# Inputs laid out by partition on the host, and the first modulation in four blocks of four, in a two-layer decoder step on one core

## The reference

```python
mod = jax.nn.silu(c) @ w_ada + b_ada
shift, scale, gate = jnp.split(mod, 3, axis=-1)
h = _rmsnorm(x, g_norm) * (1.0 + scale[:, None, :]) + shift[:, None, :]
cols = jnp.split(h @ w_in, np.cumsum(COL_SIZES)[:-1].tolist(), axis=-1)
...
y = x + gate[:, None, :] * (o @ w_out)
```

## Time and profile before

| | us |
|---|---|
| median of 3 runs | 2353.13 (2352.44 to 2353.47) |
| the profiled execution, first to last instruction (its span) | 2351.4 |
| its own time beside the span | not recorded apart from the three runs; the median lies 1.7 above the span |
| TensorE busy in the whole span | 2296.5 |
| TensorE busy in the first 126 us | 88.8 |
| start of the first pair block | 73.2 |
| end of the three first tiles (start of the next tile) | 131.8 |

### The profile page before, as it was taken

One profiled execution on the slowest core, in us unless ns is written; L12 is line 12 of the kernel. 1 busy time (PEld: TensorE's weight loads), 2 busy tenths in 40 slices (PEclk: granted clock), 3 DMA queues, 4 the chain that ended last, 5 costly groups with the idle time before them and its releaser, 6 DMA issues.

```text
span 2351.4 us, 50350 instructions
## 1 busy us (share of the span) xinstructions
PE 2296.5 (98%) x21251; PEld 2174.7 (92%) x21251; DVE 1283.2 (55%) x2499; ACT 753.7 (32%) x1219; POOL 938.6 (40%) x668
## 2 busy tenths in 40 slices
PE   5899999999999999999999999999999999999998
PEld 3799999999999999998888999999999999999998
DVE  5465666677776333442127566567767744345444
ACT  2243332333333333421114333233333333334111
POOL 2143343444333444453333333343333344346552
PEclk8999999999999999999999999999999999999999
DMA  9972333555554434368887233355554434433443
GB/s 365 352 230 76 92 92 109 156 155 155 155 155 123 114 102 110 101 194 257 247 283 215 74 92 92 92 155 155 156 158 106 125 98 109 116 95 109 109 120 107
DMA packets 473482, 347.22 MB, mean 148 GB/s; under 512 B 18701, under 2 KB 417513, under 8 KB 471937
## 3 DMA queue, kind: packets, MB, share of 16 engines
q1 hardware_dynamic: 473258, 344.02, 49.9%
HBM read 312.07 MB, written 32.09 MB: 146 GB/s over the span
## 4 chain that ended last, share of the span: by engine, by line
PE 90%; DVE 4%; DMA 3%; DVEq 1%; issue 1%; ACT 1%; POOL 1%; SPq 0%; ACTq 0%; POOLq 0%
PE pj L722 72%; PE mx L728 3%; DMA rows<-in_w_ada 2%; PE mx L1087 2%; PE mx L1113 2%; PE mx L843 1%; PE mx L1101 1%; PE mx L809 1%; PE pj L1220 1%; PE mx L1065 1%; PE mx L1115 1%; PE mx L1105 1%; DVE t L1598 1%; PE mx L990 1%; DMA rows<-in_x_prompt 1%
## 5 line engine op out<-in xcount | busy, mean ns | idle before, releaser
L722 PE MATMUL pj<-hh,whi 128*128 128x260 f32 x4928 | 1419.9, 288 | 7.9 <-DVE hl L1598 7.6
L690 POOL TENSOR_TENSOR wlo<-raw,whi 128x512 fp32r<-128x512 f32 x632 | 893.0, 1444 | 1311.7 <-ACT whi L1302 1311.7
L722 PE MATMUL pj<-hl,whi 128*128 128x260 f32 x4928 | 1393.3, 283 | 0.0
L722 PE MATMUL pj<-hh,wlo 128*128 128x260 f32 x4928 | 1390.7, 282 | 0.0
L722 PEld LDWEIGHTS pj<-hh,whi 128*128 128x128 f32 x4928 | 929.4, 189 | 52.5 <-issue 47.1
L722 PEld LDWEIGHTS pj<-hl,whi 128*128 128x128 f32 x4928 | 929.1, 189 | 0.0
L722 PEld LDWEIGHTS pj<-hh,wlo 128*128 128x128 f32 x4928 | 928.6, 188 | 0.0
L1302 ACT ACTIVATE whi<-raw 128x2048 fp32r<-128x2048 f32 x158 | 302.9, 1919 | 252.0 <-PE pj L722 174.2
L1302 ACT ACTIVATE xv<-pj 128x260 f32<-128x260 f32 x188 | 64.7, 383 | 388.0 <-PE pj L722 387.8
L1598 DVE SCALAR_TENSOR_TENSOR o<-pj,mod,t 128x260 f32<-128x260 f32 (+1 forms) x56 | 24.6, 480 | 231.1 <-PE pj L722 215.5
L1302 ACT ACTIVATE t<-t 128x520 f32<-128x520 f32 (+1 forms) x125 | 78.9, 631 | 170.9 <-DVEq L1852 124.3
(11 more groups left out here) (304 smaller groups left out, 2329.8 us busy)
## 6 DMA issues: line engine op xcount, KB each, us to landing
raw<-in_w_in SPq DMA_DIRECT2D x256, 512.0 KB, 5.3
raw<-in_w_out SPq DMA_DIRECT2D x64, 512.0 KB, 5.5
lev<-in_w_ada SPq DMA_DIRECT2D x90, 256.0 KB, 4.9
rows<-in_w_ada SPq DMA_DIRECT2D x22, 1024.0 KB, 12.1
lev<-in_w_ada SPq DMA_DIRECT2D x39, 512.0 KB, 6.0
out<-ss SPq DMA_DIRECT2D x32, 512.0 KB
xv<-in_w_ada SPq DMA_DIRECT2D x25, 512.0 KB, 5.8
y_kept<-o SPq DMA_DIRECT2D x2, 4160.0 KB, 15.9
```

The costliest lines, as they stand in the source:

```text
L690: last = e.tensor_tensor((wlo_third if t == 2 else wlo[:, par, :])[:, cs], w[:, cs], high_of(t)[:, cs].bitcast(F32), ALU.subtract)
L722: last = e.matmul(pj[:, 2 * par + b, 0:HALF], w[:, par, kb * P:(kb + 1) * P], x[:, kb, b * HALF:(b + 1) * HALF], start=(kb == 0 and m == 0 ...
```

## The change

The host now arranges the inputs before the launch. x, c and the parameters come with the model dimension on the partitions, so the transposes, their copies and their semaphores are gone. Every weight tile of `w_in` and `w_out` lies as 8 KB per partition and is one load where it was two loads of rows of 512 bytes. The pieces of the first modulation lie as 8 KB per partition; they were rows of 4 KB (the first 16) and 2 KB. x is loaded in four parts with a semaphore each, and `square` begins with the first.

The first modulation is made in four blocks of four k blocks. Before there were blocks of 8, 4 and 4, the first with 16 pieces. Now each has 8 pieces, 4 of shift and 4 of scale, and the order on TensorE is by block. The making of `lmask` moves behind the second block. The load of the third tile moves from behind piece 15 to behind piece 9. The next layer's parameters are loaded once the gates of layer 0 are made.

```diff
-FIRST_BLOCKS = ((0, 8), (8, 4), (12, 4))
+FIRST_BLOCKS = ((0, 4), (4, 4), (8, 4), (12, 4))
+FIRST_K = 4
...
-        piece_slot = [6, 7, 8, 9, 4, 5, 0, 1, 2, 3, 6, 7, 8, 9, 4, 5, 2, 3, 6, 7, 8, 9, 2, 3, 7, 8, 9, 3, 7, 8, 9, 3]
+        piece_slot = [0, 4, 1, 5, 2, 6, 3, 7, 8, 9, 1, 5, 2, 6, 3, 7, 8, 9, 2, 6, 3, 7, 8, 9, 3, 7, 8, 9, 3, 7, 8, 9]
...
                 e.wait_ge(lo_done, t - 1)
-                for b in range(2):
-                    e.dma_start(raw[:, 2 * par + b, :].rearrange("p (k n) -> p k n", k=KB // 2),
-                                src[:, b * KB // 2:(b + 1) * KB // 2, :]).then_inc(raw_in[par], 16)
+                e.dma_start(raw[:, 2 * par:2 * par + 2, :].rearrange("p a b -> p (a b)"), src).then_inc(raw_in[par], 16)
...
+            e.dma_start(t1[:, 0:9 * KB], c_cols_d).then_inc(c_in, 16)
             e.dma_start(cst[:], cst_d).then_inc(const_in, 16)
...
+            for j in range(4):
+                ks = slice(j * KB // 4, (j + 1) * KB // 4)
+                e.dma_start(o[:, ks, :].rearrange("p k t -> p (k t)"),
+                            x_cols[:, j * KB // 4 * TOK:(j + 1) * KB // 4 * TOK]).then_inc(x_in[j], 16)
             params(0)
             first_tiles(0)
             for p in range(FIRST_PIECES):
                 first_piece(p)
                 if p == 11:
                     e.dma_start(levf[:, 0:LEVELS * 128], lm_d).then_inc(lm_in, 16)
-                if p == 15:
+                if p == 9:
...
                 if l == 0:
-                    params()
-                    for p in range(16):
+                    for p in range(8):
                         first_piece(p)
-                        if p == 9:
+                        if p == 5:
                             block_columns(0)
-                        if p == 12:
+                        if p == 6:
                             norm(0)
                     block_columns(1)
...
+                    for kb in range(4):
+                        pair_block(kb)
+                        first_piece(8 + kb)
+                    first_piece(12)
+                    block_columns(2)
+                    first_piece(13)
+                    first_piece(14)
                     e.wait_ge(lo_done, 3)
                     third_block(0)
                     third_block(1)
+                    first_piece(15)
                     third_block(2)
                     block_columns(3)
                     third_block(3)
+                    for block in (1, 2):
+                        for kb in range(4 * block, 4 * block + 4):
+                            pair_block(kb)
+                            first_piece(8 + 8 * block + kb - 4 * block)
+                        for kb in range(4 * block, 4 * block + 4):
+                            third_block(kb)
+                            first_piece(12 + 8 * block + kb - 4 * block)
+                            if kb == 4 * block:
+                                block_columns(2 * block + 2)
+                        block_columns(2 * block + 3)
                     for kb in range(12, KB):
                         last = pair_block(kb)
```

More of the change, by code:

```diff
@@ L440, in first_piece @@
                     e.wait_ge(piece_used, earlier[-1] + 1)
[L441 to L449, removed]
+                e.dma_start(at, ada_first[p]).then_inc(piece_in[piece_slot[p]], 16)
+            e.dma_start(t1[:, 0:9 * KB], c_cols_d).then_inc(c_in, 16)
             e.dma_start(cst[:], cst_d).then_inc(const_in, 16)
[L452 to L455, removed]
+            for j in range(4):
+                ks = slice(j * KB // 4, (j + 1) * KB // 4)
+                e.dma_start(o[:, ks, :].rearrange("p k t -> p (k t)"),
+                            x_cols[:, j * KB // 4 * TOK:(j + 1) * KB // 4 * TOK]).then_inc(x_in[j], 16)
             params(0)
@@ L632, in _ @@
                 loaded = 4
-                load(t + 3, 1, wo[:, :, 3 * P:4 * P])
+                load(t + 3, 1, wo_tiles[l, 3])
                 if l == 0:
@@ L785, in first_piece @@
                         e.wait_ge(mod_made, u - 1)
-                    for x in range(ks):
-                        w = piece_at[piece_slot[p]].rearrange("p (k c j n) -> p k j c n", k=ks, j=4, n=P)[:, x]
+                    for x in range(FIRST_K):
+                        w = piece_at[piece_slot[p]].rearrange("p (k j n) -> p k j n", k=FIRST_K, j=4)[:, x]
                         for j in range(4):
-                            last = e.matmul(mx[32 * j:32 * j + 32, 2 + which, 0:n].rearrange("p (c n) -> p c n", n=P),
-                                            sct[:, ks * i + x, :], w[:, j], start=(i == 0 and x == 0), stop=(p == pieces - 1 and x == ks - 1))
+                            last = e.matmul(mx[32 * j:32 * j + 32, 2 + which, 0:n], sct[:, FIRST_K * i + x, :], w[:, j],
+                                            start=(i == 0 and x == 0), stop=(p == pieces - 1 and x == FIRST_K - 1))
                     last.then_inc(piece_used, 1)
@@ L978, in _ @@
                 if l == 0:
-                    for kb in range(10, KB):
+                    for kb in range(12, KB):
                         last = third_block(kb)
@@ L1230, in _ @@
                             out_part(n, part)
-                        if l == 0 and (n, part) == (10, 3):
-                            e.wait_ge(gate_ready, 1)
-                            params_next()
                         if l == 0:
@@ L1721, in _ @@
                         e.drain()
+                    if l == 0 and part == 1:
+                        e.wait_ge(lm_in, 16)
+                        ts(lmask[:], levf[:, 0:LEVELS * 128], 0.5, None, ALU.is_gt).then_inc(lm_taken, 1)
                 e.memset(x0[:, 0:PAD], 0.0)
```

201 lines of the change are left out of this document (64 added, 137 removed).

## The result

| kernel | median, us | single runs | ratio to before, 95% interval |
|---|---|---|---|
| before | 2353.13 | 2352.32 to 2356.22 (19) | |
| after | 2356.88 | 2355.32 to 2360.22 (19) | 1.0015 [1.0009, 1.0022] |

The changed kernel is 3.75 us (0.15%) slower.

What follows compares the result with a forecast made beforehand. Loads were taken to bound the opening until the first pair block, then TensorE's own queue. Opening 2.0 us earlier plus 0.4 for transposes gave 2353.1 - 2.4 = 2350.7 us, range 2348.5 to 2355.

Steps and rivals of the forecast that it cites:

- The three chains: Between the opening's blocks, take to hl takes 4.65 us each; TensorE waits for hl 11 to 13 us in all.
- the rival of a clock that doesn't fall: In the opening's three stalls the clock stays full, so 5.2 us more are won: 2345.5; chance 0.20.
- The later tiles' layout: Behind the opening, tile loads get faster but TensorE has no wait for them, so nothing is gained.
- the predicted 430: Load rate in the opening, GB/s, taken between 410 and 455; the first block's 15.1 MB take 35.1 us.
- I take 46.0: Start of the first pair block in us, against 73.2 before; 46.5 at the low clock, 44.1 at full clock.
- The root is ready at about 41.5: Ahead of the first pair block, norm's products can begin one square earlier, so its root is ready at about 41.5 us.
- I charge each 1.7, together 5.2: Clock loss after the opening's three stalls of 3.5 to 4.7 us; bounds nothing and 2.4 each.
- The next tile starts without a wait, since it did before.: End of the opening: last block priced as 5.9 + 4 x 0.76 = 8.9 us; end with clock loss at 129.8.
- Shift the rest by the difference.: Everything after the opening is TensorE back to back in the same order, shifted by the opening's new end, 2.0 us earlier.
- the 0.4 of the two transposes: The two transposes of the next layer's parameters go: 0.46 us busy, 0.4 us gained.
- Slots hold: Piece 28 needs piece 24 used, about 95.5 us, and is wanted at 105; one load takes 2.4 us plus latency.
- The rival of slow loads: In the opening the new layout moves 340 GB/s, ending it at 141.7 us: 2362.6; decides below some 355; chance 0.03.

Runs made afterwards that it cites:

- the second execution: The changed kernel profiled once more without an edit: this execution took 2357.67 us, span 2355.8; median of that rerun 2358.07 us.
- `e3_filler`: Changed kernel plus 6, 8 and 8 products of 256 columns that nothing reads, in the three stalls before pair blocks 4, 8 and 12: 2351.03 us.
- those of the first: The first profiled execution of the changed kernel, without an edit: 2360.21 us, span 2358.3.
- the layouts alone: Changed kernel with its new layouts kept, but blocks of 8, 4 and 4 and the TensorE order of before: 2348.36 us, ratio 0.9978.

## Why the prediction was wrong

*Confirmed.* The opening is bound by TensorE's own queue behind the first pair block: with a full clock the blocks lasted 23.1, 23.1 and 8.9 us (10.5 less the wait for `whi`) where the steps said 23.2, 23.1 and 8.9. The three chains stand uncovered, 3.3 to 4.0 us each, 11.2 us together, within the 11 to 13 forecast. The clock falls behind each of them, and the rival of a clock that doesn't fall is excluded by the 0.50 and 0.70 rows. The Trainium skill (TensorE: Matmul & The Clock Gate, "What's actually happening") says that the slow clock comes back after idleness; the rows of 0.50 behind the stalls agree. The later tiles' layout does nothing. Loads moved 420 GB/s for the predicted 430.

*Failed, with what it measured in place of the prediction's number:*

- **"I take 46.0" for the first pair block.** It is 48.3 and 48.8, outside the bounds given: 2.3 to 2.8 us. "The root is ready at about 41.5" was the wrong step: it was ready at 43.8 and 44.2. The squares ended 0.6 later than forecast, but norm's products stand behind piece 6 and began only at 40.2, where the forecast had 36.4. By 430 GB/s and 2.5 us piece 5 was to land near 32.7 and piece 6 near 35.2; TensorE saw piece 5 at 35.9, took it at the low clock, and began piece 6 at 38.4, at the low clock too (0.50 from 36 to 39 us). By 38.42 the DMA engines had moved 14.9 MB, though piece 6 ends at 14.1 MB of the queue, so a load is seen some 2 us after its share of the bytes; the rest is the rate, 413 GB/s counted from 2.5 us. Norm itself was quicker than forecast, 3.6 and 3.9 us instead of 5.1, since the clock was at 1.00 from 40 or 41 us on. I had the load's latency at its start and not at its landing, and I let norm begin when its data was there, not when its place in the queue came.
- **"I charge each 1.7, together 5.2"** for the clock. The blocks of the second execution are 2.5, 1.5 and 1.3 us longer than those of `e3_filler`, together 5.3, as charged; those of the first 2.6, 2.3 and 2.6, together 7.5, of which 0.5 is the wait for piece 31. The medians give 5.9. The term was right in kind and small by 0.7 in the median.
- **The next tile starts without a wait, since it did before.** It waits 1.5 us for `whi`. I priced the last block as TensorE's work alone and left out that ScalarE has 4.3 us to do before the next tile, which the last third blocks cover; the change left 3.1 us of them. The experiment that put six there shows the wait gone, but the time then went into a wait for piece 31, so a repair of this alone brings nothing.
- **"Shift the rest by the difference."** From the next tile's start to the end the difference grew by 2.3 us in the second execution and 1.9 in the first, where 0.4 less was forecast. 0.9 to 1.1 of it lie between 151 and 211 us, 0.7 to 0.95 of that in the gate projection, with its wait for issue of 0.3 to 0.6; 0.4 at the first use of `xv` at 143 us, which waits 0.38 us for VectorE; 1.2 in the last stores, which land late in some executions and not in others (0.1 in the changed kernel with the 98 transposes). From 211 us to the last products it shrank by 0.2 and 0.7; whether the 0.4 of the two transposes is in that no run shows by itself. Why the projection and the stores differ stays open.
- **"Slots hold"**, the third block: nearly so in the changed kernel (0.54 us before piece 31 in one execution, none in the other), but only since the stalls kept TensorE late. With them covered the slots do not hold.

Three slips in the prediction's working weigh little: the earlier trace rows show norm's first products as four in 2.10 us, not two; a block with its pieces adds up to 18.6 and not 18.5; and 1.5 + 2.0 above the forecast is 2354.2, where the range was given to 2355.

The sum for the second execution against the forecast: 2.3 at the start, 0.3 in the first block, 0.1 for the clock, 1.5 for `whi`, less 0.1 in the blocks themselves, that is 4.1 at the next tile (133.88 for 129.8), and 2.7 behind it: 6.8 for a span of 2355.8, where 2349.0 was forecast.

The rival of slow loads ended on the slower side too, but its mechanism is not this: 420 GB/s are far above its 355. What made the time longer than forecast was none of the priced rivals but four small terms of one sign: the late start, the clock, the uncovered wait for `whi`, and the stretch behind the opening. And the gain that the forecast counted on from the early start was small to begin with, 2.0 us, and less than the 6.4 us by which the layouts alone brought the next tile forward.

## What to carry to other kernels

An earlier start of the main work is worth nothing by itself when the same engine must still do the rest: here 20 us earlier came with 8.5 us more (7.4 of which the order alone took off again), since each small block brings one more chain of other engines, and TensorE waits through it and then runs slowly. Before splitting work into more blocks, count for each chain what is queued behind its last input, and for the end of the stage what the *other* engines have to do before the next stage; then hold that much work back. And once a wait is covered, look for which wait stands next (here the slots of the late pieces), since that bounds what the cover can bring.

## What the runs showed of the hardware that I had not expected

- Work that nothing reads can pay: 22 products in three stalls of 3.3 to 4.0 us took 5.9 us off (2356.88 to 2351.03), with the granted clock at 1.00 behind them instead of 0.50.
- TensorE can wait for "issue" in a run of short products, here 128 products of 12 weight columns, in all twelve profiles with the new layouts and without added transposes, for 0.3 to 1.7 us, and in none of the four others, the kernel before among them. 98 unread transposes some 150 us earlier removed it in two kernels. Every kernel has such waits in other products too (1.0 us in the kernel before), and one had 0.9 us in a piece. The cause stays open.
- The single runs of the changed kernel lie within 4.9 us of each other, those of before within 3.9, most of them within 1.3. Two executions of one kernel differed by 1.6 us in what they lost by slow products behind stalls of the same length (6.95 and 5.32 us, the wait for piece 31 left out).
